# Product-key expert layers: 80 keys weighted in the first stage instead of 64, 48 in the second, and four value tiles loaded early into idle buffers

## The chip, the cores and the metric

The kernel runs on one core of one Trainium2 chip. The metric is the time of one execution on the device in microseconds (us). The core has a matrix engine (TensorE, PE in the rows, with PEld for its weight loads), VectorE (DVE), ScalarE (ACT), GpSimd (POOL) and SyncE (SP), which here issues the loads of weight tiles. The engines run side by side and wait for one another on semaphores.

## The reference, cut to what matters

The kernel computes a network of several layers over 256 tokens of width 1024: a first block, an attention layer, an expert layer, a second attention layer, a second expert layer and a last norm. The change touches only the two expert layers. Each of them computes, for a token `x` (normed):

```python
q = (xc @ w_q).reshape(t, PEER_HEADS, 2, PEER_QDIM // 2)        # 8 heads, 2 halves of 128
sc = jnp.einsum('thpc,hpnc->thpn', q, sub_keys)                  # 128 scores per half
v_half, i_half = lax.top_k(sc, PEER_TOPK_HALF)                   # 16 best of each half
cand = v_half[:, :, 0, :, None] + v_half[:, :, 1, None, :]       # 16 x 16 sums
cand_idx = i_half[:, :, 0, :, None] * PEER_NKEYS + i_half[:, :, 1, None, :]
top_s, pos = lax.top_k(cand, PEER_TOPK)                          # 16 best sums of each head
expert = jnp.take_along_axis(cand_idx, pos, axis=-1)
g = jax.nn.softmax(top_s, axis=-1)
act = jax.nn.gelu(jnp.einsum('thkd,td->thk', u_tab[expert], xc))
return jnp.einsum('thk,thkd->td', g * act, v_tab[expert])
```

There are 128 x 128 experts, so `u_tab` and `v_tab` have 16384 rows each.

## The kernel before, in words

The kernel doesn't gather for most tokens. For 192 of the 256 tokens (`DENSE`) it computes every expert: the first stage multiplies the whole table U, tile by tile, with the tokens and applies Gelu, the hidden values are then multiplied by the weight of each expert (zero for those not picked), and the second stage multiplies them with the whole table V. A tile is 128 x 1024 values, 512 KB, and holds the experts of one first key; each stage has 128 tiles ("keys" below). The other 64 tokens (`GATHERED`) are done by gathering rows: 64 gathers of rows of U (128 x 4 KB each, `row_dot` L2250) and 64 of rows of V (`row_value` L2255). These 128 items lie between the other work of VectorE, in the order that `take(upto)` L2646 and the list `TAKEN` L2297 write out by hand. GpSimd issues gather n when item n - 8 has been taken (eight buffers `gbuf`).

First stage, per key (`experts` L2376): eight matmuls 128 x 192 in fp32 (L2383). SP loads a tile into one of four ring slots as soon as the tile that used the slot is done. ScalarE applies Gelu to each pair of keys (L2494) into `hidden`.

Weights: `one_hots` L2261 builds on VectorE, for a group of 8 tokens, one-hot rows in fp16: `is_first` (L2268), `hot_second` (L2270), and `hot_first` (L2274, twice: `is_first` times the high and the low part of the weight). `weights` L2277 multiplies them on TensorE, 16 matmuls of 128 x 64 per group (L2282), and `weigh` L2287 multiplies the product from PSUM into `hidden` (L2290). Two buffers of each kind alternate. It is done in two halves of the keys: keys 0 to 63 in 24 groups, spread over the last 56 keys of the first stage (`FOUR_AT`, `SIX_AT`), and keys 64 to 127 in 24 groups over the first 53 keys of the second stage. The picks come from `find_picks` L2595 on VectorE. TensorE transposes them (L2392) at key 72, and VectorE turns them to fp16 (L2687 to L2691).

Second stage, per key (`values` L2405): ten matmuls 128 x 512 (fp32r: L2413, L2414, and L344 to L346 in a helper). A V tile is first split by ScalarE into a rounded part (`tile_hi`, L2481 for the first four, L2512 for the others) and by VectorE into the rest (`tile_lo`, L2705), and the hidden values are split alike (L2485, L2486 on ScalarE, L2708 on VectorE); `value_rest` L2702 is L2705 and L2708 together. VectorE stays two keys ahead (`value_rest(a + 2)`). SP loads V tile a into its ring slot: the first four when the U tile in the slot is used, the later ones when VectorE has read the tile (`load_table` L2210).

At the border of the stages ScalarE rounds V tiles 0 and 1 after the last Gelu but one, rounds the hidden values of keys 0 to 3, applies the last Gelu, and rounds V tiles 2 and 3 (L2488 to L2505). VectorE does `value_rest` of keys 0 and 1, the first group of the second half, and then waits for the last Gelu (L2713). In the first expert layer SP clears a list of semaphores between the last load of U and the first of V (L2230 to L2232).

## Time and profile before

| | |
|---|---|
| median of 3 runs | 2077.0 us (2076.82 to 2078.7) |
| profiled execution | 2068.39 us, its span 2066.6 us |
| busy share | TensorE 97%, VectorE 78%, ScalarE 42%, GpSimd 19% |
| first expert layer | first stage from 530.5 us to 880.0 us, second to 1199.6 us |
| second expert layer | first stage from 1392.7 us to 1743.1 us, second to 2056.9 us |

A row of the timeline holds the start, the time that it took, the engine, the line, the operation, and after xN how many of the kind were merged; in brackets stands how long the engine had been idle before it, and what ended the wait. A busy time of TensorE is no measure of how near it is to its peak, since a matmul is counted until its end and the next one begins before that. The distance between starts is. The time around the span is 1.8 us in the profiled execution, and this execution was 8.6 us shorter than the median of the runs.

### The profile page before, as it was taken

The numbers are of one execution on the slowest core, as the hardware profiler recorded it, in microseconds if no ns is written. First come the engines' busy times: TensorE is split into PE (matmuls) and PEld (weight loads), VectorE is DVE, ScalarE is ACT, GpSimd is POOL, SyncE is SP. The second block draws the span as 40 slices with busy tenths as digits, with TensorE's granted clock in tenths as the row PEclk, the third lists the DMA queues.
The fourth block names the chain that finished last, engine by engine and source line by source line (L and its number), as shares of the span: only waits on it lengthen the run. The fifth ranks groups of instructions, "written<-read, shape, count | busy, mean of one in ns | idle before, by whom it ended". The sixth has DMA issues, their size and how long they took to land.

```text
span 2066.6 us, 35237 instructions
## 1 busy us (share of the span) xinstructions
PE 2007.3 (97%) x12408; PEld 1791.5 (87%) x12408; DVE 1622.2 (78%) x3208; ACT 857.9 (42%) x1653; POOL 385.0 (19%) x262
## 2 busy tenths in 40 slices
PE   8999999999999999999999999999999999999998
PEld 6888887779999999977887887899999998778786
DVE  6899886865799276699999967639964756999997
ACT  6557454545101100055565666531101002555665
POOL 0000000000024233303243100000352322232440
PEclk9999999999999999999999999999999999999999
DMA  6554344415389989867799853335998988678995
GB/s 258 198 203 163 114 139 156 138 67 174 133 337 341 368 321 327 300 241 229 262 351 356 294 184 117 113 117 195 391 353 309 346 306 317 224 243 281 371 377 181
DMA packets 132634, 511.17 MB, mean 247 GB/s; under 512 B 15004, under 2 KB 15132, under 8 KB 129856
## 3 DMA queue, kind: packets, MB, share of 16 engines
q1 hardware_dynamic: 95680, 375.81, 51.7%
q0 software_dynamic: 36864, 134.23, 17.6%
q8 instruction: 47, 0.77, 0.1%
q14 instruction: 43, 0.35, 0.1%
HBM read 508.94 MB, written 1.05 MB: 247 GB/s over the span
## 4 chain that ended last, share of the span: by engine, by line
PE 64%; DVE 16%; DMA 5%; issue 2%; ACT 2%; SPq 0%; DVEq 0%; ACTq 0%
PE bank L2383 30%; PE bank L344 8%; PE bank L346 8%; PE bank L345 8%; DVE tile_lo L2705 5%; DMA wbuf<-in_peer_v 3%; PE bank L2413 3%; PE bank L2414 3%; DVE x_tok L2258 2%; DMA wbuf<-in_peer_u 2%; PE bank L2282 1%; DVE w_parts L2708 1%; DVE e_hot_first L2274 1%; DVE e_hidden L2290 1%; DVE tile_lo L274 1%
## 5 line engine op out<-in xcount | busy, mean ns | idle before, releaser
L2383 PE MATMUL bank<-h_dense,wbuf 128*128 128x192 f32 x4096 | 679.7, 327 | 3.7 <-ACT e_stage L2467 2.4
L2383 PEld LDWEIGHTS bank<-h_dense,wbuf 128*128 128x128 f32 x4096 | 664.2, 190 | 6.0 <-issue 4.9
L2512 ACT ACTIVATE tile_hi<-wbuf 128x1024 fp32r<-128x1024 f32 x248 | 263.0, 1060 | 246.1 <-DMA wbuf<-in_peer_v 202.3
L2705 DVE TENSOR_TENSOR tile_lo<-wbuf,tile_hi 128x1024 fp32r<-128x1024 f32 x256 | 311.0, 1215 | 37.7 <-ACT tile_hi L2512 27.4
L2244 POOL DMA_INDIRECT e_gbuf<-in_peer_v,e_row_at x128 | 227.1, 1774 | 484.3 <-DVE x_tok L2258 445.8
L2494 ACT ACTIVATE e_hidden<-bank 128x384 f32<-128x384 f32 x128 | 62.7, 490 | 603.2 <-PE bank L2383 603.2
L2244 POOL DMA_INDIRECT e_gbuf<-in_peer_rows,e_row_at x128 | 155.8, 1218 | 470.1 <-DVE e_dots L2252 239.0
L2413 PE MATMUL bank<-tile_hi,w_parts 128*128 128x512 f32 x512 | 208.5, 407 | 11.1 <-DVE w_parts L2708 10.4
L274 DVE TENSOR_TENSOR tile_lo<-wbuf,tile_hi 128x1024 fp32r<-128x1024 f32 (+2 forms) x117 | 140.3, 1212 | 80.1 <-ACT tile_hi L266 79.2
L2414 PE MATMUL bank<-tile_lo,w_parts 128*128 128x512 f32 x512 | 200.4, 391 | 0.0
L344 PE MATMUL bank<-tile_hi,w_parts 128*128 128x512 f32 x512 | 200.1, 391 | 0.0
L345 PE MATMUL bank<-tile_lo,w_parts 128*128 128x512 f32 x512 | 200.0, 391 | 0.0
L346 PE MATMUL bank<-tile_hi,w_parts 128*128 128x512 f32 x512 | 199.8, 390 | 0.0
L355 PE MATMUL bank<-a_parts,tile_hi 128*128 128x512 f32 x512 | 177.8, 391 | 0.0
L2252 DVE CUSTOM_DVE_ANT_0 e_gbuf<-e_gbuf,x_gathered 128x1024 f32<-128x1024 f32 x128 | 152.2, 1217 | 18.5 <-DMA e_gbuf<-in_peer_rows,e_row_at 18.1
L2258 DVE SCALAR_TENSOR_TENSOR x_tok<-e_gbuf,e_acts,x_tok 128x1024 f32<-128x1024 f32 x128 | 163.4, 1276 | 1.3
L266 ACT ACTIVATE tile_hi<-wbuf 128x1024 fp32r<-128x1024 f32 (+2 forms) x117 | 121.9, 1046 | 66.4 <-PE bank L346 58.9
L354 PE MATMUL bank<-a_parts,tile_hi 128*128 128x256 f32 x512 | 143.8, 281 | 0.6 <-DVE tile_hi L681 0.5
L2413 PEld LDWEIGHTS bank<-tile_hi,w_parts 128*128 128x128 f32 x512 | 96.5, 188 | 42.4 <-DVE w_parts L2708 24.7
L2290 DVE SCALAR_TENSOR_TENSOR e_hidden<-bank,e_hidden 128x512 f32<-128x512 f32 x96 | 65.6, 683 | 80.4 <-PE bank L2282 80.4
L2238 POOL MEMSET x_tok<- 64x1024 f32 x2 | 1.9, 948 | 667.1 <-DVE e_stage L2549 667.1
L561 ACT ACTIVATE tile_hi<-wbuf 128x512 fp32r<-128x512 f32 x144 | 89.9, 630 | 66.6 <-PE bank L355 62.6
(391 smaller groups left out, 3500.3 us busy)
## 6 DMA issues: line engine op xcount, KB each, us to landing
wbuf<-in_peer_u SPq DMA_DIRECT2D x256, 512.0 KB, 5.7
wbuf<-in_peer_v SPq DMA_DIRECT2D x256, 512.0 KB, 5.0
wbuf<-in_w_in SPq DMA_DIRECT2D x16, 2048.0 KB, 7.7
wbuf<-in_peer_q SPq DMA_DIRECT2D x32, 512.0 KB, 3.8
wbuf<-in_hyb_in SPq DMA_DIRECT2D x16, 512.0 KB, 3.7
wbuf<-in_mla_uq SPq DMA_DIRECT2D x9, 512.0 KB, 3.4
wbuf<-in_mla_in SPq DMA_DIRECT2D x8, 528.0 KB, 4.2
wbuf<-in_w_v SPq DMA_DIRECT2D x2, 2048.0 KB, 7.3
```

The costliest lines, as they stand in the source:

```text
L274: nc.vector.tensor_tensor(g["tile_lo"][:, slot, 0:width], g["ring"][:, slot, 0:width], g["tile_hi"][:, slot, 0:width].bitcast(F32), ALU.su ...
L344: nc.tensor.matmul(out, hi[:, cols], other_hi, start=start, stop=False, **kw)
L345: nc.tensor.matmul(out, hi[:, cols], other_lo, start=False, stop=False, **kw)
L346: return nc.tensor.matmul(out, lo[:, cols], other_hi, start=False, stop=stop, **kw)
L355: return nc.tensor.matmul(out, hi[:, cols], parts, start=False, stop=stop, skip_group_check=True)
L2244: nc.gpsimd.indirect_dma_start(out=gbuf[:, b, :], out_offset=None, in_=(U_ROWS if n < SHARED else V_ROWS)[:, :], in_offset=bass.IndirectOf ...
L2258: nc.vector.scalar_tensor_tensor(out=x[:, 1, :], in0=gbuf[:, n % GBUFS, :], scalar=acts[:, n:n + 1], in1=x[:, 1, :], op0=ALU.mult, op1=ALU ...
L2383: last = nc.tensor.matmul(bank[:, j // 2 % 2, j % 2 * S:j % 2 * S + DENSE], ring[:, slot, k * P:(k + 1) * P], h_dense[:, k, :], start=(k = ...
L2413: nc.tensor.matmul(sums(1, c), both, tile_hi[:, slot, cols], start=False, stop=False, skip_group_check=True)
L2414: last = nc.tensor.matmul(sums(1, c), both, tile_lo[:, slot, cols], start=False, stop=False, skip_group_check=True)
L2512: nc.scalar.activation(tile_hi[:, slot, 0:D], ring[:, slot, 0:D], ACT.Copy).then_inc(hi_done, 1)
L2705: nc.vector.tensor_tensor(tile_lo[:, slot, 0:D], ring[:, slot, 0:D], tile_hi[:, slot, 0:D].bitcast(F32), ALU.subtract).then_inc(lo_done, 1)
```

## The change

- Weights: `PARTS` says 80 keys in 32 groups of 6 tokens for the first stage, and 48 keys in 24 groups of 8 tokens for the second. The groups of the first lie in 40 keys from key 80 on (after four of five keys), and 8 keys without a group follow. Those of the second lie in the first 72 keys, one after every third. The transposes of the picks move from key 72 to key 80.
- The two multiplications L2274 become one over an operand of twice the size. High and low part lie interleaved, so that a matmul reads its moving operand with a step of four fp16 values and not of two.
- Items: 86 instead of 78 are taken in the first stage, 6 instead of 10 beside the groups of the second, and the last 36 within 46 keys (72 to 118) instead of 40 within 60 (56 to 116). The Gelu of the gathered dots (L2502) becomes two, after pairs 46 and 51 instead of 54.
- Border: the first four V tiles go to `tile_raw`, which lies where `tile_lo` lies. SP issues these loads directly behind the last of U (in the first expert layer behind the clears), with no wait. The ring loads of V tiles 4 to 7 wait for the last four U tiles. ScalarE rounds V tiles 0 to 3 and the hidden values of keys 0 to 3 ahead of the last Gelu, and only when all four tiles have landed (`v_first`).
- Picks: of the 16 x 16 sums only 17 rows of 8 are kept, and the decoding of places has some more small operations. The zeroing of 64 rows of `x` moves from GpSimd to VectorE, ahead of the first group. The transposes take 128 rows where they took 64.

```diff
+            "tile_raw": nc.alloc_sbuf_tensor_at("tile_raw", [P, SLOTS, TILE], F32, offset=wbuf_at + 2 * BUF),
...
+    PARTS = ((0, 80, 6), (80, 48, 8))
...
-        load_table(sp, V, M_V, used, lo_done)
+        for a in range(SLOTS):
+            sp.dma_start(v_raw[a], V[a:a + 1, :, :].rearrange("a p c -> p (a c)")).then_inc(v_first, DMA)
+        for j in range(SLOTS, STEP):
+            sp.wait_ge(used, M_V + j - STEP + 1)
+            load_slot(sp, V, j, (M_V + j) % SLOTS)
+        load_rest(sp, V, M_V, lo_done)
...
-        for part in range(2):
-            made = nc.vector.tensor_tensor(hot_first[b][:, part, :, :, :], is_first[b][:, :, :, :], pairs(2 + part, HALF), ALU.mult)
-        made.then_inc(hots_done, 1)
+        nc.vector.tensor_tensor(weighted_first, first.unsqueeze(3).to_broadcast([P, pairs, keys, 2, 2]),
+                                pick_parts[:, pairs * n:pairs * n + pairs, :, :].unsqueeze(2).to_broadcast([P, pairs, keys, 2, 2]),
+                                ALU.mult).then_inc(hots_done, 1)
...
-    FOURS, SIXES, WEIGHING = 3, 2, 7
-    FIRST_WEIGHING = ROUNDS - WEIGHING
-    FOUR_AT = {0: 0, 2: 1, 4: 2, 6: 3}
-    SIX_AT = {0: 0, 2: 1, 5: 2, 7: 3, 10: 4, 12: 5}
-    TAKEN, LAST_TAKE = (16, 30, 36, 78, 88), 116
-    EXPS_AT, ACTS_AT = (16, 30), 54
+    FIRST_WEIGHING, FIRST_LOOPS, FIRST_LOOP = FIRST_KEYS // STEP, 2, 20
+    FIRST_AT = {j: n for n, j in enumerate(j for j in range(FIRST_LOOP) if j % 5 < 4)}
+    SECOND_LOOPS, SECOND_LOOP = 3, 24
+    SECOND_AT = {3 * n: n for n in range(8)}
+    WEIGHING = SECOND_LOOPS * SECOND_LOOP // STEP
+    TAKEN, LAST_TAKE = (16, 30, 36, 86, 92), 118
+    EXPS_AT, ACTS_AT, ACTS = (16, 30), (46, 51), (slice(0, 48), slice(48, SHARED))
...
         def rounded_v(a):
-            slot = (M_V + a) % SLOTS
-            act.wait_ge(ring_loaded[slot], DMA * ((M_V + a) // SLOTS + 1))
-            nc.scalar.activation(tile_hi[:, slot, 0:D], ring[:, slot, 0:D], ACT.Copy).then_inc(hi_done, 1)
+            act.wait_ge(v_first, SLOTS * DMA)
+            nc.scalar.activation(tile_hi[:, (M_V + a) % SLOTS, 0:D], v_raw[a], ACT.Copy).then_inc(hi_done, 1)
...
-        for f in range(HALF):
+        for f in range(NKEYS // 2):
+            if f == NKEYS // 2 - 1:
+                act.wait_ge(weighted, 2 + NGROUPS[0])
+                for a in range(SLOTS):
+                    rounded_v(a)
+                    hidden_rounded(a, a)
             act.wait_ge(used, M_U + 2 * f + 2)
-            if f == HALF - 1:
-                act.wait_ge(weighted, 2 + NGROUP)
-                for a in range(SLOTS):
-                    hidden_rounded(a, a)
...
+        nc.vector.memset(x[LOW, 1, :], 0.0).then_inc(picks_kept, 1)
-        dve.wait_ge(bank_free, 2 + HALF // 2)
+        dve.wait_ge(bank_free, 2 + FIRST_KEYS // 2)
```

## Rows read from the trace of the kernel before

**Rows 1.** Timeline of TensorE, end of the first layer's first stage.
```profile
857.32 0.64 PE L2282 MATMUL bank<-e_hot_first,e_hot_second 128*128 128x64 f16 x16
857.81 8.04 PE L2383 MATMUL bank<-h_dense,wbuf 128*128 128x192 f32 x48
...
865.68 0.64 PE L2282 MATMUL bank<-e_hot_first,e_hot_second 128*128 128x64 f16 x16
...
871.45 0.65 PE L2282 MATMUL bank<-e_hot_first,e_hot_second 128*128 128x64 f16 x16
```

**Rows 2.** Timeline of TensorE, second stage: steady keys, last groups, ends.
```profile
1022.76 0.65 PE L2282 MATMUL bank<-e_hot_first,e_hot_second 128*128 128x64 f16 x16
...
1176.93 0.39 PE L2413 MATMUL bank<-tile_hi,w_parts 128*128 128x512 f32 x1
...
1199.37 0.39 PE L346 MATMUL bank<-tile_hi,w_parts 128*128 128x512 f32 x1
...
1884.21 0.65 PE L2282 MATMUL bank<-e_hot_first,e_hot_second 128*128 128x64 f16 x16
...
2056.68 0.39 PE L346 MATMUL bank<-tile_hi,w_parts 128*128 128x512 f32 x1
```

**Rows 3.** Chain in order of time (start, us, what), SP's queue at the border.
```profile
869.19 0.33 SPq L2208
...
875.13 0.34 SPq L2208
```

**Rows 4.** Timeline of ScalarE and TensorE, start of each layer's second stage.
```profile
879.07 1.06 ACT L2481 ACTIVATE tile_hi<-wbuf 128x1024 fp32r<-128x1024 f32 x1 [3.76 <-DMA wbuf<-in_peer_v]
...
884.50 0.80 PE L2413 MATMUL bank<-tile_hi,w_parts 128*128 128x512 f32 x1 [4.52 <-DVE w_parts L2708]
...
1744.52 0.50 PE L2413 MATMUL bank<-tile_hi,w_parts 128*128 128x512 f32 x1 [1.39 <-DVE w_parts L2708]
```

**Rows 5.** Busy time by stretch (PE, PEld, DVE, ACT, POOL, then granted clock, DMA share, GB/s).
```profile
885.00:890.00 5.00, 5.00 (x27) 3.74 (x26) 5.00 (x11) 3.25 (x6) 0.00 (x0) 0.50 0.57 193
...
1050.00:1100.00 50.00, 49.92 (x214) 39.31 (x213) 45.49 (x56) 30.61 (x63) 20.42 (x14) 1.00 0.99 364
1950.00:2000.00 50.00, 49.92 (x218) 40.22 (x217) 48.16 (x59) 31.76 (x66) 26.08 (x15) 1.00 1.00 379
```

**Rows 6.** Timeline of VectorE in the first stage, one group and its items.
```profile
738.39 0.42 DVE L2268 TENSOR_TENSOR e_is_first<-e_wide,e_picks_T 128x512 f16<-128x512 f16 x1
738.73 0.68 DVE L2270 TENSOR_TENSOR e_hot_second<-e_wide,e_picks_T 128x1024 f16<-128x1024 f16 x1
739.34 0.75 DVE L2274 TENSOR_TENSOR e_hot_first<-e_is_first,e_picks_T 128x512 f16<-128x512 f16 x2
741.27 0.69 DVE L2290 SCALAR_TENSOR_TENSOR e_hidden<-bank,e_hidden 128x512 f32<-128x512 f32 x1 [1.18 <-PE bank L2282]
741.87 1.22 DVE L2252 CUSTOM_DVE_ANT_0 e_gbuf<-e_gbuf,x_gathered 128x1024 f32<-128x1024 f32 x1
...
743.01 1.22 DVE L2252 CUSTOM_DVE_ANT_0 e_gbuf<-e_gbuf,x_gathered 128x1024 f32<-128x1024 f32 x1
```

**Rows 7.** Timeline of VectorE in the second stage: a value rest, an item.
```profile
1035.61 1.22 DVE L2705 TENSOR_TENSOR tile_lo<-wbuf,tile_hi 128x1024 fp32r<-128x1024 f32 x1
...
1037.01 1.28 DVE L2258 SCALAR_TENSOR_TENSOR x_tok<-e_gbuf,e_acts,x_tok 128x1024 f32<-128x1024 f32 x1
1038.20 1.22 DVE L2705 TENSOR_TENSOR tile_lo<-wbuf,tile_hi 128x1024 fp32r<-128x1024 f32 x1
```

**Rows 8.** Timeline of VectorE and TensorE where the first group is made.
```profile
720.34 0.36 DVE L2687 TENSOR_SCALAR e_picks_T<-bank 128x192 f16<-128x192 f32 x1 [17.35 <-PE bank L2335]
...
723.28 0.66 PE L2282 MATMUL bank<-e_hot_first,e_hot_second 128*128 128x64 f16 x16 [0.37 <-DVE e_hot_first L2274]
```

**Rows 9.** The page's costliest groups (busy, mean ns), the zeroing on GpSimd.
```profile
L2238 POOL MEMSET x_tok<- 64x1024 f32 x2 | 1.9, 948 | 667.1 <-DVE e_stage L2549 667.1
```

More of the change, by code:

```diff
@@ L2127, in expert_layer @@
     ROUNDS = NKEYS // STEP
-    HALF = NKEYS // 2
-    GROUP = 8
+    PARTS = ((0, 80, 6), (80, 48, 8))
+    FIRST_KEYS = PARTS[0][1]
     WEIGHT_ONE = 4096.0
-    NGROUP = DENSE // GROUP
+    NGROUPS = [DENSE // group for start, keys, group in PARTS]
     TURN_BANKS = (0, 1, 4, 5)
@@ L2277, in weights, with hots @@
-    def weights(pe, half, n, b):
-        pe.wait_ge(hots_done, 2 * (NGROUP * half + n + 1))
-        pe.wait_ge(weighted, NGROUP * half + n + 1)
-        for m in range(GROUP):
+    def hots(half, b):
+        start, keys, group = PARTS[half]
+        first = is_first[b][:, 0:group * keys].rearrange("p (i a m) -> p i a m", a=keys, m=2)
+        weighted_first = hot_first[b][:, 0:2 * group * keys].rearrange("p (i a w m) -> p i a w m", a=keys, w=2, m=2)
+        second = hot_second[b][:, 0:group * NKEYS].rearrange("p (i a m) -> p i a m", a=NKEYS, m=2)
+        return first, weighted_first, second
@@ new lines, in one_hots, with by_pairs @@
+    def one_hots(dve, half, n):
+        start, keys, group = PARTS[half]
+        pairs = group // 2
+        first, weighted_first, second = hots(half, n % 2)
+        tokens = slice(group * n, group * n + group)
+        def by_pairs(rows, keys):
+            return picks_T[:, rows, tokens].rearrange("p (i m) -> p i m", m=2).unsqueeze(2).to_broadcast([P, pairs, keys, 2])
+        nc.vector.tensor_tensor(first, wide[:, start:start + keys, :].unsqueeze(1).to_broadcast([P, pairs, keys, 2]),
+                                by_pairs(0, keys), ALU.is_equal).then_inc(first_done, 1)
+        nc.vector.tensor_tensor(second, wide[:, :, :].unsqueeze(1).to_broadcast([P, pairs, NKEYS, 2]),
+                                by_pairs(1, NKEYS), ALU.is_equal).then_inc(hots_done, 1)
+        dve.wait_ge(first_done, NGROUPS[0] * half + n + 1)
+        nc.vector.tensor_tensor(weighted_first, first.unsqueeze(3).to_broadcast([P, pairs, keys, 2, 2]),
+                                pick_parts[:, pairs * n:pairs * n + pairs, :, :].unsqueeze(2).to_broadcast([P, pairs, keys, 2, 2]),
+                                ALU.mult).then_inc(hots_done, 1)
@@ L2281, in weights @@
+    def weights(pe, half, n, b):
+        start, keys, group = PARTS[half]
+        first, weighted_first, second = hots(half, b)
+        pe.wait_ge(hots_done, 2 * (NGROUPS[0] * half + n + 1))
+        pe.wait_ge(weighted, NGROUPS[0] * half + n + 1)
+        for m in range(group):
             for part in range(2):
-                last = nc.tensor.matmul(bank[:, 2 + b, m * HALF:(m + 1) * HALF], hot_second[b][:, m // 2, :, m % 2],
-                                        hot_first[b][:, part, m // 2, :, m % 2],
+                last = nc.tensor.matmul(bank[:, 2 + b, m * keys:(m + 1) * keys], second[:, m // 2, :, m % 2],
+                                        weighted_first[:, m // 2, :, part, m % 2],
@@ L2499, in scalar @@
                 exps(1, 0)
-            if f == ACTS_AT:
-                act.wait_ge(gather_used, GATHER_0 + SHARED)
-                nc.scalar.activation(acts[:, :], dots[:, :], ACT.Gelu).then_inc(exps_done, 1)
-            if f >= HALF - 2:
-                for a in range(2):
-                    rounded_v(2 * (f - HALF + 2) + a)
+            if f in ACTS_AT:
+                part = ACTS[ACTS_AT.index(f)]
+                act.wait_ge(gather_used, GATHER_0 + part.stop)
+                nc.scalar.activation(acts[:, part], dots[:, part], ACT.Gelu).then_inc(exps_done, 1)
         def value_tile(r, j):
@@ L2716, in vector @@
             value_rest(a + 2)
[L2717 to L2719 removed]
+            if a < WEIGHING * STEP and a % SECOND_LOOP in SECOND_AT:
+                if done < NGROUPS[1] - 1:
                     one_hots(dve, 1, done + 1)
```

144 lines of the change are left out of this document (71 added, 73 removed).

## The prediction, made before the changed kernel was run

> **What bounds the kernel now.** I read the page first: TensorE is busy 97% of the span, so only what TensorE does, or what makes it wait, can move the end. As busy time hides gaps, I then read distances between starts on TensorE's timeline. In the first stage three keys and one group of weight matmuls take 865.68 - 857.32 = 8.36 us, two keys and a group 871.45 - 865.68 = 5.77 us [rows 1]. So a key costs 2.6 us and a group 0.56 us, of which 0.49 us lies between its start and that of the next key's matmuls, 30 ns for each of 16. In the second stage ten steady keys last from 1176.93 to 1199.37 plus one matmul, 22.65 us [rows 2], so 2.265 us a key. With these two prices I measured what the second stages lose. From the first value matmul to the 24th group lie 53 keys and 23 groups, by the prices 120.0 + 11.3 = 131.3 us. They took 1022.76 - 884.50 = 138.3 us in the first expert layer and 1884.21 - 1744.52 = 139.7 us in the second: 7.0 and 8.4 us lost [rows 2, 4]. From there to the end one group and 75 keys should take 170.4 us and took 176.8 and 172.7 us: 6.4 and 2.3 us lost [rows 2]. Between the stages TensorE idles 4.52 and 1.39 us [rows 4]. That is all there is to win: 4.5 + 7.0 + 6.4 and 1.4 + 8.4 + 2.3, 30 us in both layers. The first stages run nearly without gaps.
>
> Three causes stand behind the loss. VectorE: per group of the second stage it does two value rests (1.40 us each, from 1035.61 to 1037.01 [rows 7]), one-hots of 0.34 + 0.61 + 0.67 us and a weighing of 0.60 us [rows 6], together 5.0 us, plus an item of 1.19 us [rows 7] at every sixth key. TensorE needs 2 x 2.265 + 0.49 = 5.02 us. So VectorE binds there. The clock: after the idle 4.5 us of the first layer the granted clock is 0.50, which is 1.2 GHz, from 885 to 890 us [rows 5], and the first key takes twice its time (2.6 us more, part of the 7.0). Late in the stage: transfers. With two items in three keys the queues must bring 1.667 tiles of 0.524 MB in 2.265 us, 386 GB/s, and the rows show 364 and 379 GB/s at a share of 0.99 and 1.00 [rows 5].
>
> **The change, part by part, for each layer.**
>
> *Weight matmuls.* 24 groups of 16 with 64 columns become 32 of 12 with 80, and 24 of 16 with 64 become 24 of 16 with 48. If columns set the 30 ns, 16 more cost 6.7 ns at 2.4 GHz: a group of the first stage costs 12 x 37 ns + 0.07 = 0.51 us, so 32 x 0.51 - 24 x 0.56 = +2.9 us, and the second stage saves 24 x 16 x 6.7 ns = 2.6 us. If loading the stationary operand sets it, 32 x (0.36 + 0.07) - 13.4 = +0.4 us, and nothing is saved. Both give +0.4, which I take. The ends are -2.2 (load price in the first, column price in the second) and +2.9 (the reverse). The Trainium skill (TensorE: Matmul & The Clock Gate, "Wait — 56ns, not 53.3ns?") gives N / 2.4 GHz + 2.5 ns with a floor of 25 ns. By that the estimate would be +2.5 and -1.6, net +0.9 us a layer. At 64 columns it says 29 ns and the trace 30 ns.
>
> *First stage, VectorE.* Where the row shows 0.34 us for 512 elements and 0.61 for 1024, the price is 0.07 us + elements / 1920 per us [rows 6]. A new group: 480 (0.32) + 768 (0.47) + 960 (0.57) + weighing of 480 at one element a cycle (0.57) = 1.93 us. Items: 28 dots at 1.14 (741.87 to 743.01 [rows 6]) and 22 values at 1.19 [rows 7], 58.1 us over 32 groups, 1.82 a group. Sum 3.75 us. TensorE: 1.25 keys and a group, 3.25 + 0.51 = 3.76 us. Equal, so VectorE has no reserve left, where it had 1.18 us of idle time in a group before [rows 6]. The start costs more: from the first conversion to the first group lie 2.94 us, 0.37 of them waited for by TensorE [rows 8]. Zeroing on VectorE is added; GpSimd needs 0.95 us [rows 9], I take 1.1, and the first one-hots are 0.25 us shorter: 0.85 more. I add 0.25 us for uneven gaps between groups. So +1.1 us, between +0.3 and +4.
>
> *What has no price at the end.* The shorter search for picks ends in the 17.35 us that VectorE waits for the transposes [rows 8]. Without that cover its few us would count. Wider transposes are 11 times some 0.06 us, and the split Gelu removes a wait on VectorE that TensorE didn't feel. Earlier gathers only fill buffers earlier.
>
> *Border.* SP has queued: last load of U, in the first layer the clears, then four loads of V. The clears stay: 869.19 to 875.13, 5.9 us [rows 3]. The last U load is issued 10.3 us before the stage's end T (four keys remain). First layer: V is issued from T - 4.4. One tile took 3.9 us (875.13 to 879.07 [rows 3, 4]), three more follow at 0.524 MB / 370 GB/s = 1.4 us, so all have landed at T + 3.3. ScalarE waits for all four; behind its wait stand only the last Gelu and all rounding. Rounding 1.06, VectorE's 1.14 + 0.36 and some handover give 2.6 us: TensorE starts at T + 5.9, against 4.5 now. The clock falls as before: 2.6, and 0.3 for small waits. Sum 8.8, before 4.5 + 7.0 = 11.5: -2.7 us. Second layer: V is issued at T - 9.9, behind the last U tile, landed at about T - 1.2, TensorE starts at T + 1.4, as now. Then VectorE is late three times: the first group's one-hots (0.5), rests of key 2 (0.15) and of key 3 (0.9), as it waits for the last Gelu behind 6.2 us of rounding on ScalarE. Sum 3.0, before 1.4 + 8.4 = 9.8: -6.8 us. In both I take nothing for the rest of the 72 keys: VectorE needs 3 x 1.40 + (0.27 + 0.60 + 0.47 + 0.47) + 0.3 = 6.3 us, and TensorE 3 x 2.265 + 0.4 = 7.2 us. Ends: 2 us either way in each layer, by the landing time.
>
> *Late items.* From key 72 there are 36 items in 46 keys, and the first 28 of them each call a gather: 0.783 a key. VectorE needs 1.40 + 0.783 x 1.19 = 2.33 us against 2.265, at most 3 us in all, most of it covered by its lead of two keys: loss 1 us, the lower end. Transfers: 36 + 28 tiles in 36 keys, 33.6 MB in 81.5 us = 412 GB/s. At 364 GB/s that lasts 92.2 us, at 379 88.5 us: losses 10.7 and 7.0, the upper ends. Full slots and eight full buffers at the start absorb some. I take 8.0 and 5.5, near the transfer bound, since the stretch already loses at 386 GB/s: +1.6 and +3.2 us.
>
> *Sum.* First layer 0.4 + 1.1 - 2.7 + 1.6 = +0.4; second 0.4 + 1.1 - 6.8 + 3.2 = -2.1. Together -1.7 us. The profiled execution would go from 2068.4 to 2066.7 us; it was 8.6 us below the median, so I apply the same difference to the median: 2077.0 - 1.7 = 2075.3 us.
>
> **The rivals.**
>
> *The late stretch loses no more than VectorE's 1 us.* Then 7.0 and 4.5 us more are won: -13.2, 2064 us; half of it gives 2069. For it: the second layer lost only 2.3 us at a demand of 386. Against it: the share of 0.99 to 1.00.
>
> *Transfers at their full price, and matmuls at +2.9.* 0.4 + 2.5 + 2.7 = +5.6 and -2.1 + 2.5 + 1.5 = +1.9: +7.5, 2084.5 us.
>
> *Slower by one mechanism: the joined multiplication runs at one element a cycle.* It is the only operation of a new shape, with four dimensions and two of them repeated. It would take 0.07 + 1.00 instead of 0.57 us. From 3.76 us a group VectorE sets the pace of the weighing part of the first stage; 4.25 us is above it by 0.49, 32 times in two layers: +31, 2107 us. Against it: both old inputs also step by pairs of adjacent values, and the rows show two elements a cycle.
>
> *The wider step of the moving operand costs TensorE.* At half the column rate: 32 x 12 x 37 ns + 24 x 16 x 23 ns = 23 us a layer, 2121 us. Against it: at the present step of 4 bytes the 30 ns leave 3 ns above the columns. No row shows 8 bytes. The Trainium skill (SBUF — State Buffer, on cachelines of 16 bytes) holds two accesses to a line to be enough for full rate, and a step of 8 bytes makes just two; one more would cost.
>
> **How the numbers follow.** Forecast 0.42 (own range 2071 to 2080), late stretch free 0.36, full transfer and matmul price 0.12, slow multiplication 0.06, slow step 0.04. The likeliest gives 2075.3. For 8 in 10 I reach into the two neighbours: 2063 to 2085, which leaves out 0.10 above by the last two and as much again in the tails. About 0.2%, 4.2 us, can be told from no change. Faster: 0.36 + 0.06 = 0.42. Slower: 0.10 + 0.10 + 0.01 = 0.21. Within: 0.37.
>
> **What would show it.** Right: weight groups of 0.51 us in the first stage and about 0.4 in the second, three keys and a group 7.2 us apart from key 4 to 72, no idle VectorE between groups of the first stage, 5 to 6 us idle with a clock of 0.50 after it in the first layer and under 2 us in the second, and key distances of 2.4 to 2.5 us from key 72 to 108 with ScalarE waiting for V tiles. Wrong: groups of the first stage 4.2 us apart, an early start of the second stage in the first layer, or late keys at 2.27 us.

## The result, and the profile after

The changed kernel takes 2120.7 us (median, 2117.1 to 2122.5) where the kernel before takes 2077.9 us beside it. The ratio is 1.0194 with an interval of 1.0163 to 1.0226, so it is slower by 43 us. Its profiled execution took 2121.6 us, with a span of 2119.8 us, against 2068.4 and 2066.6 before. The profile before is 9.5 us shorter than the median beside which the changed kernel was timed, so a difference of these two profiles overstates the change. A second comparison of the same kernel (experiment 5 below) gave 1.0176 [1.0144, 1.0208] and a profiled span of 2104.7 us. The forecast was 2075.3 us, the range ended at 2085, and the mechanism that decided, at 2121 us, had been given a chance of 0.04.

The weight matmuls of the first stage answer [rows 1]. Timeline of TensorE, changed kernel:

```profile
755.27 1.05 PE L2301 MATMUL bank<-e_hot_first,e_hot_second 128*128 128x80 f16 x12 [1.12 <-DVE e_hot_first L2290]
756.14 2.82 PE L2406 MATMUL bank<-h_dense,wbuf 128*128 128x192 f32 x16
758.79 1.05 PE L2301 MATMUL bank<-e_hot_first,e_hot_second 128*128 128x80 f16 x12
```

Twelve matmuls of 80 columns take 756.14 - 755.27 = 0.87 us up to the next key's first, 72.5 ns each. Before, sixteen of 64 took 0.49 us, 30 ns each. In the second stage the same view answers [rows 2, 4]:

```profile
913.31 0.80 PE L2435 MATMUL bank<-tile_hi,w_parts 128*128 128x512 f32 x1 [5.54 <-DVE w_parts L2739]
...
917.75 0.94 PE L2301 MATMUL bank<-e_hot_first,e_hot_second 128*128 128x48 f16 x16
918.51 0.62 PE L2435 MATMUL bank<-tile_hi,w_parts 128*128 128x512 f32 x1
...
1796.07 0.80 PE L2435 MATMUL bank<-tile_hi,w_parts 128*128 128x512 f32 x1 [2.47 <-DVE w_parts L2739]
```

Sixteen matmuls of only 48 columns take 0.76 us here and 0.72 us in the steady part: 45 ns each, where fewer columns than before should have taken less than 30. VectorE is not the one behind it. Its timeline answers [rows 6]:

```profile
758.20 0.40 DVE L2285 TENSOR_TENSOR e_is_first<-e_wide,e_picks_T 128x480 f16<-128x480 f16 x1
758.52 0.55 DVE L2287 TENSOR_TENSOR e_hot_second<-e_wide,e_picks_T 128x768 f16<-128x768 f16 x1
758.99 0.64 DVE L2290 TENSOR_TENSOR e_hot_first<-e_is_first,e_picks_T 128x960 f16<-128x960 f16 x1
759.88 0.66 DVE L2310 SCALAR_TENSOR_TENSOR e_hidden<-bank,e_hidden 128x480 f32<-128x480 f32 x1 [0.25 <-PE bank L2301]
```

The joined multiplication of 960 elements is busy for 0.64 us, as the 1024 elements of the second one-hot were before (0.68), and 0.57 us pass to the next operation where one follows at once, as forecast: it kept the fast rate. And VectorE now waits for TensorE again (0.25 us).

All stages, from distances between starts on TensorE's timeline (us; first and second expert layer). "Group" is from a group's first matmul to the next key's. "Idle" is counted from the last matmul of the first stage, taken as long as the distance between its like, so it is 0.1 to 0.2 us more than in the brackets of the rows:

| kernel | first stage | idle at border | second stage | group, first / second stage | both layers |
|---|---|---|---|---|---|
| before | 349.4, 350.3 | 4.6, 1.5 | 315.1, 312.4 | 0.49 / 0.49 | 1333.3 |
| changed, first profile | 375.7, 371.0 | 5.7, 2.6 | 316.4, 314.1 | 0.87 / 0.72 | 1385.5 |
| changed, second profile | 364.9, 366.1 | 6.1, 2.7 | 314.8, 314.4 | 0.87 / 0.72 | 1368.9 |
| changed, step of 4 bytes | 354.8, 353.6 | 6.6, 3.4 | 307.2, 304.8 | 0.44 / 0.42 | 1330.3 |
| best (experiment 5) | 353.5, 353.0 | 0, 0 | 302.9, 302.9 | 0.45 / 0.42 | 1312.3 |

The first profile of the changed kernel holds 16.6 us in these layers that the second does not. They are the subject of experiment 5.

### The profile page after: what moved, and what is told of

The parts are those of the page before. It is cut to its first block, busy times and chain, and to the rows that moved or that the text cites. A ratio compares the mean times of both kernels' runs of the same rounds, so it can differ in the third digit from the quotient of the medians.

```text
span 2119.8 us, 35225 instructions
## 1 busy us (share of the span) xinstructions
PE 2051.8 (97%) x12408; PEld 1838.7 (87%) x12408; DVE 1604.7 (76%) x3192; ACT 860.7 (41%) x1655; POOL 364.1 (17%) x260
## 4 chain that ended last, share of the span: by engine, by line
PE 75%; DVE 6%; DMA 4%; issue 2%; ACT 2%; another core or an unknown queue 1%; SPq 0%; DVEq 0%; ACTq 0%
PE bank L2406 28%; PE bank L345 10%; PE bank L347 10%; PE bank L346 10%; PE bank L2435 5%; PE bank L2436 5%; PE bank L2301 4%; DMA wbuf<-in_peer_u 2%; DMA wbuf<-in_peer_v 1%; DVE tile_lo L275 1%; DVE x_tok L2264 1%; DMA tile_raw<-in_peer_v 1%; PE bank L2391 1%; DVE tile_lo L2736 1%
## 5 line engine op out<-in xcount | busy, mean ns | idle before, releaser
L2406 PE MATMUL bank<-h_dense,wbuf 128*128 128x192 f32 x4096 | 686.8, 328 | 13.7 <-DMA wbuf<-in_peer_u 9.0
L2736 DVE TENSOR_TENSOR tile_lo<-wbuf,tile_hi 128x1024 fp32r<-128x1024 f32 x248 | 302.4, 1219 | 12.1 <-ACT tile_hi L2527 9.9
L2250 POOL DMA_INDIRECT e_gbuf<-in_peer_v,e_row_at x128 | 211.5, 1653 | 536.7 <-DVE x_tok L2264 510.1
L267 ACT ACTIVATE tile_hi<-wbuf 128x1024 fp32r<-128x1024 f32 (+2 forms) x117 | 121.9, 1046 | 64.2 <-PE bank L347 59.6
L2310 DVE SCALAR_TENSOR_TENSOR e_hidden<-bank,e_hidden 128x480 f32<-128x480 f32 (+1 forms) x112 | 68.6, 612 | 73.9 <-PE bank L2301 68.9
L682 DVE TENSOR_TENSOR tile_hi<-wbuf,tile_hi 128x512 fp32r<-128x512 f32 x144 | 98.4, 688 | 24.5 <-ACT tile_hi L562 23.6
```

What stands on the lines that cost most here:

```text
L2250: nc.gpsimd.indirect_dma_start(out=gbuf[:, b, :], out_offset=None, in_=(U_ROWS if n < SHARED else V_ROWS)[:, :], in_offset=bass.IndirectOf ...
L2406: last = nc.tensor.matmul(bank[:, j // 2 % 2, j % 2 * S:j % 2 * S + DENSE], ring[:, slot, k * P:(k + 1) * P], h_dense[:, k, :], start=(k = ...
L2736: nc.vector.tensor_tensor(tile_lo[:, slot, 0:D], raw, tile_hi[:, slot, 0:D].bitcast(F32), ALU.subtract).then_inc(lo_done, 1)
```

## The experiments

**1. The step of the moving operand, undone and done alone.** The theory after the result: TensorE reads the interleaved operand with a step of four fp16 values (8 bytes), and that halves its column rate. The rival: the new split of keys, the border or the transfers cost the 43 us. The first kernel is the changed one with high and low part apart again, so that the step is 4 bytes:

```diff
-        weighted_first = hot_first[b][:, 0:2 * group * keys].rearrange("p (i a w m) -> p i a w m", a=keys, w=2, m=2)
+        weighted_first = hot_first[b][:, 0:2 * group * keys].rearrange("p (w i a m) -> p w i a m", w=2, a=keys, m=2)
...
-                                        weighted_first[:, m // 2, :, part, m % 2],
+                                        weighted_first[:, part, m // 2, :, m % 2],
```

> The changed kernel with one thing put back: high and low part of the weight lie apart again and are made by two multiplications, so a weight matmul reads its moving operand with a step of 2 fp16 values (4 bytes) and not of 4 (8 bytes). Groups, keys, items and border stay as changed. Theory 1 (the step halves the column rate): a group of 12 x 80 falls from 0.87 us to about 0.45 us and one of 16 x 48 from 0.72 to about 0.40 us, 32 x 0.42 + 24 x 0.32 = 21 us a layer, 42 us in all, so about 2078 us. Theory 2 (80 columns in 32 groups are dear in themselves, whatever the step): groups stay at 0.87 us and 0.72 us, within 5 us of 2121. Theory 3 (VectorE sets the pace): its work grows by 0.07 us a group, so a little slower than 2121.

Measured: 2068.7 us, ratio 0.9998 [0.9971, 1.0025]. Timeline of TensorE in this kernel:

```profile
752.81 0.60 PE L2300 MATMUL bank<-e_hot_first,e_hot_second 128*128 128x80 f16 x12
753.26 2.84 PE L2405 MATMUL bank<-h_dense,wbuf 128*128 128x192 f32 x16
755.93 0.61 PE L2300 MATMUL bank<-e_hot_first,e_hot_second 128*128 128x80 f16 x12
...
904.98 0.58 PE L2300 MATMUL bank<-e_hot_first,e_hot_second 128*128 128x48 f16 x16
905.39 0.48 PE L2434 MATMUL bank<-tile_hi,w_parts 128*128 128x512 f32 x1
```

The groups are down to 0.45 us (37 ns a matmul) and 0.41 us (26 ns). A key and a group of the first stage take 3.12 us instead of 3.53. With nothing changed but the layout and one multiplication made two, the whole slowdown is gone. (The two kernels were timed in different comparisons, each beside the kernel before, so their ratios are set side by side and not their times.)

The second kernel is the one before with only the interleaved layout and the joined multiplication:

```diff
-        for part in range(2):
-            made = nc.vector.tensor_tensor(hot_first[b][:, part, :, :, :], is_first[b][:, :, :, :], pairs(2 + part, HALF), ALU.mult)
+        nc.vector.tensor_tensor(hot_first[b][:, :, :, :, :], is_first[b][:, :, :, :].unsqueeze(3).to_broadcast([P, PAIRS, HALF, 2, 2]),
+                                pick_parts[:, PAIRS * n:PAIRS * n + PAIRS, :, :].unsqueeze(2).to_broadcast([P, PAIRS, HALF, 2, 2]),
...
-                                        hot_first[b][:, part, m // 2, :, m % 2],
+                                        hot_first[b][:, m // 2, :, part, m % 2],
```

> The kernel before with one thing of the change: the two multiplications joined, high and low part interleaved, so the step of the moving operand is 8 bytes; 64 columns, 16 matmuls a group, 24 groups in each half as before. Theory 1: a matmul of 64 columns goes from 30 ns to about 58 ns, a group from 0.49 to 0.93 us, 48 x 0.44 = 21 us a layer, about 2119 us. Theory 2 (column count and grouping): no change, 2077 us. Theory 3 (VectorE): VectorE saves 0.07 us a group, no change.

Measured: 2101.8 us, ratio 1.0143 [1.0108, 1.0178]. Timeline of TensorE, first stage:

```profile
762.12 1.14 PE L2283 MATMUL bank<-e_hot_first,e_hot_second 128*128 128x64 f16 x16
763.08 5.11 PE L2384 MATMUL bank<-h_dense,wbuf 128*128 128x192 f32 x30
```

A group takes 0.96 us, twice the 0.49 of [rows 1]. The first stages grow by 11.1 and 10.4 us, which is the full price of 24 x 0.47 = 11.3. The second stages grow by 1.6 and 8.0 only. Their first 72 keys grow by 7.4 and 6.4 us of 11.3: there VectorE was the slower one, and part of the slower matmuls lies beside its work. The rest is no saving of that kind. In the first layer the idle at the border is 1.8 us and not 4.6, and keys 72 to 118 take 104.7 us where the profile before has 110.5, with the same items in the same order. One profile of each kernel doesn't tell why. So the layers lose 28 us where 42 were expected from the two stages (45 by the measured group). Both directions agree: the step is the cause.

**2. The step by itself.** A kernel of its own with 48 matmuls in a row for each setting, between single matmuls of 512 columns (line 50) as marks.

> Only matmuls, nothing of the reference: for each of 48, 64, 80 and 128 columns of fp16, 48 matmuls in a row with a moving step of 1, 2, 3, 4, 6 and 8 values, then a step of 4 at three other offsets, two steps of the stationary operand, and fp32 with steps of 1, 2 and 4. Theory 1 says that the time from start to start jumps between a step of 2 and of 4 values, from columns / 2.4 GHz to twice that (64 columns: 30 to about 57 ns; 80 columns: 37 to 72 ns). If it is a question of 16-byte lines touched in a row, a step of 3 should lie between and 8 should be twice 4 again; if it is a simple rate of half for any step over 4 bytes, 3, 4, 6 and 8 are alike. Theory 2 says all steps are alike at a given column count.

Timeline of TensorE. A setting lasts from its first start to that of the mark behind it:

```profile
22.30 1.36 PE L45 MATMUL bank<-mh,wh 128*128 128x48 f16 x48
23.50 0.38 PE L50 MATMUL bank<-mh,wh 128*128 128x512 f16 x1
...
27.06 2.33 PE L45 MATMUL bank<-mh,wh 128*128 128x48 f16 x48
29.21 0.40 PE L50 MATMUL bank<-mh,wh 128*128 128x512 f16 x1
...
62.48 2.00 PE L45 MATMUL bank<-mh,wh 128*128 128x80 f16 x48
64.31 0.38 PE L50 MATMUL bank<-mh,wh 128*128 128x512 f16 x1
...
67.46 3.68 PE L45 MATMUL bank<-mh,wh 128*128 128x80 f16 x48
70.96 0.40 PE L50 MATMUL bank<-mh,wh 128*128 128x512 f16 x1
...
121.28 3.06 PE L45 MATMUL bank<-mh,wh 128*128 128x64 f16 x48
124.16 0.40 PE L50 MATMUL bank<-mh,wh 128*128 128x512 f16 x1
```

48 columns take (23.50 - 22.30) / 48 = 25.0 ns at a step of 2 bytes and 44.8 at 8 bytes; 80 columns take 38.1 ns at 4 bytes and 72.9 at 8. In ns from start to start, with the granted clock of the stretch in brackets where it was below 0.99 (the 38.1 ns hold a first moment at the low clock; over the whole 1.83 us it was 0.96):

| step | 48 columns | 64 | 80 | 128 |
|---|---|---|---|---|
| 2 bytes | 25.0 | 53.5 (0.50) | 66.7 (0.50) | 80.0 (0.69) |
| 4 bytes | 25.0 | 45.8 (0.60); 30.2 | 38.1 | 57.9 |
| 6 bytes | 35.4 | 45.8 | 56.5 | 88.3 |
| 8 bytes | 44.8 | 59.6; 60.0 (0.51) | 72.9 | 115.6 |
| 12 bytes | 66.3 | 86.5 | 108.3 | 171.2 (0.84) |
| 16 bytes | 86.3 (0.79) | 116.0 (0.50) | 143.5 (0.50) | 226.7 (0.50) |

From 80 to 128 columns one more column costs (57.9 - 38.1) / 48 = 0.41 ns at 4 bytes, which is one cycle of 2.4 GHz, then 0.66 at 6 bytes, 0.89 at 8, 1.31 at 12 and 1.73 at 16. Up to 4 bytes the cycle sets the price. Beyond, the price is in proportion to the step, some 0.22 ns for every two bytes of it: 3 x 0.22 at 6 bytes, 4 x 0.22 at 8, 8 x 0.22 at 16. The 72.9 and 44.8 ns are those of the groups in the changed kernel (72.5 and 45). The entry of 60.0 ns is the setting from 121.28 on, with the operand one value further, and it is as long at 0.51 of the clock as its like at 1.00 (59.6). Busy time by stretch (PE, PEld, DVE, POOL, then granted clock, DMA share, GB/s):

```profile
121.40:124.13 2.73, 2.73 (x49) 2.73 (x48) 0.00 (x0) 0.00 (x0) 0.51 0.00 0
124.50:127.21 2.71, 2.71 (x49) 2.71 (x47) 0.00 (x0) 0.00 (x0) 1.00 0.00 0
```

So a wide step is limited by something that does not follow the engine's clock. Where it sits between memory and engine these runs don't tell. A very wide step also goes with a lower clock. TensorE was busy throughout, yet the granted clock fell to 0.50 four times, each time in a setting of 12 or 16 bytes, and came back to 1.00 in a setting of 2 to 8 bytes. In the same columns, 80 columns at 16 bytes and 128 at 4 bytes:

```profile
76.90:83.64 6.74, 6.74 (x49) 5.94 (x48) 0.00 (x0) 0.00 (x0) 0.50 0.00 0
...
88.20:90.83 2.63, 2.63 (x48) 2.63 (x47) 0.00 (x0) 0.00 (x0) 1.00 0.00 0
```

In the changed kernel, where groups at 8 bytes lie between other matmuls, the clock stayed at 1.00 (750 to 900 us of its second profile). (The 30.2 ns of the table are those of a setting whose stationary operand has a step of 4 bytes too.)

**3. The search for picks.** The changed kernel at a step of 4 bytes, with the old search over 16 x 16 sums:

```diff
+            work = half_scores[:, t, :, :].rearrange("p j n -> p (j n)").rearrange("p (h a b) -> p h a b", h=PH, a=PK)
...
-            after(nc.vector.tensor_tensor(sums_of[:, :, 0:PK], by_half[:, :, 0, 0:1].to_broadcast([P, PH, PK]), by_half[:, :, 1, :], ALU.add))
```

> As after_step4b, and the old search over 16 x 16 sums and the old decoding are back, so that the gathers of the first expert layer start some 4 us later again. In the changed kernel TensorE idled 3.8 us at 595 us for a U tile that SP issued 5 us late at the turn of its loop, while the gathers' first burst ran, and the clock fell behind it; that was not so before. If the earlier gathers are the cause, this kernel is 5 to 8 us faster than after_step4b. If the late issue is chance, the two are within 2 us of each other.

Measured: 2065.3 us, ratio 0.9985 [0.9962, 1.0008], against 0.9998 with the new search on the same chip. The intervals overlap, so no gain of the shorter search is seen, as forecast. In neither profile does TensorE wait 3.8 us for a U tile as it did in the changed kernel, so this pair can't tell what brought that wait (experiment 5 takes it up).

**4. The border and the late items.** Four kernels in a comparison of their own, beside a kernel before of 2080.5 us, so their ratios are compared with one another only. (All four take 217 to 222 us to their first group, where two kernels of experiments 1 and 3 take 213 to 215 with the same work, so first stages are not compared across the two. Experiment 5 comes back to this.) All have the step of 4 bytes. The first has the old border: V tiles through the ring, rounding around the last Gelu.

```diff
-        for a in range(SLOTS):
-            sp.dma_start(v_raw[a], V[a:a + 1, :, :].rearrange("a p c -> p (a c)")).then_inc(v_first, DMA)
-        for j in range(SLOTS, STEP):
-            sp.wait_ge(used, M_V + j - STEP + 1)
+        for j in range(STEP):
+            sp.wait_ge(used if j < SLOTS else lo_done, M_V + j - SLOTS + 1)
```

> after_step4b with the border of the kernel before: V tiles 0 to 3 go to the ring when their U tile is used, ScalarE rounds two of them after the last Gelu but one and two after the last. In after_step4b TensorE idles 6.6 us between the stages of the first expert layer and 3.4 us in the second (4.6 and 1.5 before), the first four keys take 11.9 and 10.9 us (13.0 and 12.0 before) and the second stages 307.2 and 304.8 us (315.1 and 312.4 before). Theory 1: the early loads gave next to nothing, since all four must land before the first is rounded; the second stage is shorter because its groups ask less of VectorE and TensorE. Then the gaps go back to 4.6 and 1.5 us, the first four keys to about 13 and 12, the rest stays, and the time is within 3 us of after_step4b. Theory 2: the early loads carry the gain of the second stage. Then the second stages go back to 312 to 315 us and the time rises by 10 us or more.

Measured: 2071.6 us, ratio 0.9953 [0.9936, 0.9969]. TensorE idles 1.5 and 1.2 us here at the borders, against 6.6 and 3.4 us with the early loads and the joint wait in experiment 1: those made the border worse. Timelines of ScalarE and TensorE, old border:

```profile
891.13 1.06 ACT L2493 ACTIVATE tile_hi<-wbuf 128x1024 fp32r<-128x1024 f32 x1 [4.14 <-DMA wbuf<-in_peer_v]
...
894.27 0.50 PE L2430 MATMUL bank<-tile_hi,w_parts 128*128 128x512 f32 x1 [1.41 <-DVE w_parts L2736]
```

The run missed what was expected of it: an idle of 4.6 us was to come back in the first layer, and it is 1.5, with the old border. In the profile of the kernel before, the second V tile was ready for ScalarE 3.5 us after the first (882.60 and 879.07 us), here 1.2 us after it (892.37 and 891.13). The second kernel of experiment 1, which has the old border and the old order of the items, shows 1.3 us (898.59 and 897.29) and an idle of 1.8 us. So a late second tile made the 4.6 us of the profile before, and neither the border nor the order of the items makes it come every time. Why it came late there is open. The forecast took these 4.5 us for a lasting loss.

In the changed kernel ScalarE waits for four tiles instead of one. Its timeline, and of the chain in order of time the three pieces ahead of it:

```profile
910.67 1.06 ACT L2497 ACTIVATE tile_hi<-tile_raw 128x1024 fp32r<-128x1024 f32 x1 [7.57 <-DMA tile_raw<-in_peer_v]
```

```profile
903.01 0.34 SPq L2238
...
903.87 0.43 SPq L2238
...
904.34 6.24 DMA tile_raw<-in_peer_v
```

The loads are issued behind the clears, from 903.01 to 904.3, and the last lands 6.24 us later. The next kernel gives each tile a semaphore of its own:

```diff
-            sp.dma_start(v_raw[a], V[a:a + 1, :, :].rearrange("a p c -> p (a c)")).then_inc(v_first, DMA)
+            sp.dma_start(v_raw[a], V[a:a + 1, :, :].rearrange("a p c -> p (a c)")).then_inc(v_each[a][0], DMA)
...
-            act.wait_ge(v_first, SLOTS * DMA)
+            act.wait_ge(v_each[a][0], DMA * v_each[a][1])
```

> after_step4b, and ScalarE waits for each of the four early V tiles by itself, not for all four. The tiles land some 1.3 us apart. Theory 1 (the joint wait makes the gap): the first rounding starts 3 to 4 us earlier in both layers, the gaps fall from 6.6 to about 3 us and from 3.4 to under 1 us, the clock doesn't fall at the second layer's border, 5 to 8 us in all. Rival: the gap is set by the issue of the loads, the first tile lands hardly before the fourth as they share the queues, and less than 2 us is won.

Measured: 2068.2 us, ratio 0.9940 [0.9917, 0.9963]. The idle of the second layer is gone, that of the first is 2.1 us, more than with the old border:

```profile
891.31 1.06 ACT L2497 ACTIVATE tile_hi<-tile_raw 128x1024 fp32r<-128x1024 f32 x1 [3.97 <-DMA tile_raw<-in_peer_v]
...
893.95 0.50 PE L2435 MATMUL bank<-tile_hi,w_parts 128*128 128x512 f32 x1 [1.94 <-DVE w_parts L2738]
```

The third kernel issues the four loads ahead of the clears as well (the same two lines moved up in SP's program).

> each_tile, and in the first expert layer SP issues the four early V tiles before it clears its list of semaphores, which takes 5.9 us, and not after. Theory 1: the gap of the first layer falls to under 1 us and no clock falls behind it, 4 to 6 us faster than each_tile, with the second layer as it was. Rival: the clears now delay the ring loads of V tiles 4 to 7 and the loss only moves there, so that keys 4 to 8 stall, no gain.

Measured: 2065.4 us, ratio 0.9929 [0.9905, 0.9952], and no idle at either border. ScalarE's timeline has the rounding begun at 886.40 and the last Gelu at 891.81, so its wait of 1.53 us is over before TensorE needs anything:

```profile
886.40 1.06 ACT L2497 ACTIVATE tile_hi<-tile_raw 128x1024 fp32r<-128x1024 f32 x1 [1.53 <-DMA tile_raw<-in_peer_v]
...
891.81 0.47 ACT L2511 ACTIVATE e_hidden<-bank 128x384 f32<-128x384 f32 x1
```

The three intervals overlap, so the traces have to tell. Idle time and first 72 keys, both layers together: 364.3 us with the joint wait (experiment 1), 355.3 with the old border, 356.1 with a wait for each tile, 352.4 with the clears moved too. So the joint wait lost 9 us, a wait for each tile alone got back to the old border and no further, and only with the clears behind the loads are 2.9 us won. Keys 72 to 118 took 2.6 us more in that last kernel than with the old border (107.3 and 107.4 against 105.8 and 106.3), which hides the gain in the total. The fourth kernel spreads the later items again:

```diff
-    TAKEN, LAST_TAKE = (16, 30, 36, 86, 92), 118
+    TAKEN, LAST_TAKE = (16, 30, 36, 84, 104), 118
```

> each_tile_clears with the items spread anew: 84 in the first stage, 20 beside the groups of the second (72 keys), and 24 instead of 36 in keys 72 to 118. Keys 72 to 118 took 106.4 and 104.9 us in after_step4b, 104.2 by their price. Theory 1 (transfers bind late): the late stretch falls to 104.3 in both layers, the 72 keys before it stay as they were since VectorE needs 7.1 us for three keys and TensorE 7.3: 2 to 3 us faster. Rival: VectorE binds in the 72 keys, which grow by more than 3 us.

Measured: 2057.1 us, ratio 0.9884 [0.9860, 0.9908]. Keys 72 to 118 take 104.3 us in both layers where they took 107.3 and 107.4 in the kernel before it; 46 keys at 2.265 us are 104.2. Its interval touches that of the kernel before it (0.9905 to 0.9908), but its five times (2055.0 to 2061.5) all lie below that kernel's six (2062.6 to 2070.3).

**5. The changed kernel and the best one, side by side.** Two things were open. In the first profile of the changed kernel SP's queue had stood still for 11.3 us in all, the longest time for 5.0 us while the first gathers ran, and TensorE idled behind it. Waits of SP's queue, changed kernel, first profile (us in total, times, longest):

```profile
SPq L2211 <- remote: 11.3, 3, 5.0
```

And the best kernel and the changed one had not been timed beside each other. Both kernels are unaltered.

> The changed kernel once more, unaltered. Open from its first profile: the queue of SyncE stood 5.0 us at a turn of its loop while the first gathers ran (from 586.5 us), TensorE idled 0.7 and 3.8 us behind it, and 223.3 us passed from the start of the first stage of the first expert layer to its first weight group, where the same kernel with a step of 4 bytes took 214.5. If the slow step is the only lasting cost, this run shows no such stop, at most 216 us to the first group, weight groups at 0.87 and 0.72 us from their start to the next matmul as before, and a ratio of 1.015 to 1.020. If the stop belongs to the order of the work in this kernel (another cause beside the step), it comes again at the same loop turn, with 220 us or more to the first group.

> Step of 4 bytes, a wait for each V tile, the clears behind the early loads, and the later items spread as before: the best kernel so far, now beside the changed kernel on one chip. By the causes named so far it is 42 us (step) plus 2 x 3 (gap at the border) plus 2 x 1.5 to 3 (late stretch) below the changed kernel, some 52 us, and its ratio to the kernel before is near 0.990. A ratio above 0.997 would mean that its gain in the first comparison came from the chip and not from the edits.

Measured: the changed kernel 2105.3 us, ratio 1.0176 [1.0144, 1.0208]; the best one 2048.6 us, ratio 0.9909 [0.9880, 0.9937]. In the second profile of the changed kernel SP has no wait of that kind, and the first groups begin 212.9 and 213.7 us after the start of the stage, where it had been 223.3 and 218.3. Of the 16.6 us between the two profiles of the changed kernel, 10.4 + 4.6 = 15.0 lie ahead of the first groups. So the stop is no lasting part of this kernel. But it was no accident of one execution either: the same wait stands in all four profiles of experiment 4, first at 581 to 585 us, where it was 586.5 in the changed kernel. The one with the old border:

```profile
SPq L2210 <- remote: 22.8, 7, 4.4
```

None of the five profiles of experiments 1, 3 and 5 that hold the whole kernel has it, nor has the profile of the kernel before. It goes with the comparison and not with the kernel. In the two comparisons where it is seen, the kernel before takes 2077.9 and 2080.5 us, in the other two 2067.8 and 2068.4; and all four times of the changed kernel are 2117.1 to 2122.5 beside the first of these and 2101.5 to 2108.4 beside the last. The ratio hardly moves, 1.0194 and 1.0176. The one profile of the kernel before has no such wait, but that execution was 8.6 us shorter than the median of its runs; whether the others held the wait is not shown. What held SP is open. The two kernels here are 56.8 us apart, with 52 expected.

Timelines of TensorE and ScalarE in the best kernel at the first border, which answer [rows 4]:

```profile
882.84 3.41 PE L2406 MATMUL bank<-h_dense,wbuf 128*128 128x192 f32 x20
885.95 0.53 PE L2435 MATMUL bank<-tile_hi,w_parts 128*128 128x512 f32 x1
```

```profile
881.71 1.06 ACT L2497 ACTIVATE tile_hi<-tile_raw 128x1024 fp32r<-128x1024 f32 x1
```

The first value matmul follows the last hidden one with no idle time, because ScalarE had begun on the first tile 4.2 us earlier. In the second stage this kernel loses nothing: 128 x 2.265 + 24 x 0.53 = 302.6 us, and it takes 302.9.

## Why the prediction was wrong, point by point

**The step that failed** is the price of the weight matmuls, "30 ns for each of 16" carried over by columns or by loads. Neither of its two prices held for the new access. The mechanism was named as a rival and held at 0.04 on two grounds: that a step of 4 bytes costs nothing, which says nothing about 8, and the rule in the Trainium skill (SBUF — State Buffer) that two accesses to a line of 16 bytes are enough for the full rate. The runs contradict that rule for a moving operand: at 6 bytes the rate is already down to 0.41 / 0.66 of the full one, at 8 bytes, two accesses to a line, to half. The rival's size was near. It gave 23 us a layer. Against the kernel with 4 bytes, both layers together, the second profile shows 1368.9 - 1330.3 = 38.6 us, 19 a layer: 10.1 and 12.5 in the first stages (32 groups, a period of 3.53 against 3.12 us, make 13.1) and 7.6 and 9.6 in the second, less 0.5 and 0.7 at the borders. That its 2121 us meet the measured 2120.7 is in part luck: 46 us for the step were too much against 38.6. "No row shows 8 bytes" was a reason to keep the chance well above 0.04. A change that alters the access of 1536 matmuls on the bounding engine has its price in doubt first of all.

**The rest of the sum came out, in part by luck.** Without the step the changed kernel is at 0.9998; the forecast of -1.7 us meant 0.9992. But its terms missed and cancelled, both layers together: the border, forecast at -9.5 us, gave -3.7, and the late items, forecast at +4.8, gave -5.8. The terms, from the row "step of 4 bytes" against "before":

- *Weight matmuls.* The two prices were columns (+2.9 in the first stage, -2.6 in the second) or loads (+0.4 and nothing). Columns set it: 37 ns at 80, 26 ns at 48. With what a group does to the key behind it, a group costs 3.117 - 2.600 = 0.517 us (0.51 forecast) where it cost 0.563, so 32 x 0.517 - 24 x 0.563 = +3.0. In the second stage it costs 0.53 us where it cost 0.60 before (5.14 us for two keys and a group where nothing waits), so -1.7. Net +1.3, taken as +0.4. The Trainium skill (TensorE: Matmul & The Clock Gate, "Wait — 56ns, not 53.3ns?"), N / 2.4 GHz + 2.5 ns and no less than 25, agrees with these runs at steps up to 4 bytes within 2.3 ns (25.0 at 48 columns, 38.1 at 80, 57.9 at 128), and its estimate of +0.9 was nearer than mine; it does not speak of the step.
- *VectorE in the first stage*, +1.1. The first stages grew by 5.4 and 3.3 us, 4.4 on average, where 2.9 + 1.1 = 4.0 was forecast at the price by columns. Right. The new operations cost what was worked out: 0.32, 0.47 and 0.57 us.
- *Joined multiplication at one element a cycle*: fell, as the rows above show.
- *Border, first layer.* Forecast 5.9 us of idle time, measured 5.7 to 6.6. Right, for the reason given: the clears, then four tiles. In the second layer 1.4 was forecast and 2.6 to 3.4 measured: tiles behind the last of U landed later than I took, inside the end of 2 us. Idle time and loss in the first 72 keys together are 8.4 and 4.3 us, where 8.8 and 3.0 were forecast. The term still missed, since the loss before, from which it was counted, held some 2.5 us a layer that were the groups' own price (below), and an idle time of 4.5 us that the same border does not show each time (experiment 4). What I did not see is that the idle time of the second layer can bring the clock down there too. Busy time by stretch in the changed kernel (PE, PEld, DVE, ACT, POOL, then granted clock, DMA share, GB/s), to set beside [rows 5], and ahead of them that of the kernel before at its second border, where the clock stayed up:

```profile
1744.50:1749.50 5.00, 4.52 (x33) 3.52 (x34) 3.58 (x7) 2.70 (x7) 0.00 (x0) 1.00 1.01 403
```

```profile
915.00:920.00 5.00, 5.00 (x29) 3.79 (x29) 4.43 (x9) 2.99 (x7) 0.00 (x0) 0.62 0.00 1
...
1797.00:1802.00 5.00, 5.00 (x30) 3.90 (x29) 4.43 (x10) 3.75 (x10) 0.00 (x0) 0.75 0.09 34
```

How long the engine idled does not decide this alone. With the step of 4 bytes the second layer's idle time was 3.24 us by the profile, and the clock stayed up. With the old search for picks it was 3.23 us, and the clock fell. With a wait for each tile it fell after 1.94 us, in the first layer. These three in this order:

```profile
1748.80:1753.80 5.00, 4.73 (x34) 3.67 (x35) 4.49 (x10) 4.60 (x12) 0.00 (x0) 1.00 0.13 48
```

```profile
1747.40:1752.40 5.00, 5.00 (x29) 3.78 (x30) 4.49 (x10) 4.14 (x10) 0.00 (x0) 0.66 0.15 59
```

```profile
893.95:898.95 5.00, 5.00 (x29) 3.82 (x30) 4.49 (x10) 4.67 (x12) 0.00 (x0) 0.66 1.03 419
```

- *Loss to VectorE in the second stage.* The gain came: the second stages at 4 bytes are 7.9 and 7.6 us shorter. It comes from one group in three keys, not from the early loads, since the old border has it too (305.3 and 305.7 us). Of the 7.0 and 8.4 us that I called lost, about 2.5 were the price of the groups themselves, which I had put at 0.49 us where they cost 0.60 with the slower start of the next key.
- *Late items.* Over-estimated. Forecast losses were 8.0 and 5.5 us, measured are 106.4 and 104.9 us for keys 72 to 118 against 104.2, so 2.2 and 0.7, and in the changed kernel's second profile 1.7 and 1.8. The wrong step was to take 364 and 379 GB/s as what the queues can give, and the 6.4 us lost in the first layer as the cost of such a demand. The kernel before with only the step widened (experiment 1) has the same items in these keys and loses 0.5 us there (and 3.7 in the second layer). The changed kernel moves more in the first layer's late keys (second profile):

```profile
1095.00:1125.00 30.00, 30.00 (x134) 24.87 (x133) 29.76 (x36) 18.00 (x39) 15.60 (x11) 1.00 1.00 379
1125.00:1155.00 30.00, 30.00 (x134) 24.83 (x133) 29.54 (x37) 17.61 (x37) 14.73 (x10) 1.00 1.01 393
1155.00:1185.00 30.00, 29.92 (x130) 23.65 (x129) 29.98 (x36) 18.73 (x39) 14.58 (x9) 1.00 1.01 394
```

With the DMA engines' share at 1.00 the rate still rose to 394 GB/s (and to 419 for 5 us at the border, in the last row of the point on the border), and TensorE waited next to nothing. VectorE is busy for 89.3 of 90 us there, so it is as near to being the bound as the transfers, as the forecast's lower end had it. No run separates the two: moving items away eases both. The best kernel asks for less in the same keys:

```profile
1070.00:1100.00 30.00, 30.00 (x134) 24.84 (x133) 26.83 (x34) 19.20 (x41) 11.76 (x7) 1.00 0.94 348
1100.00:1130.00 30.00, 30.00 (x134) 24.87 (x133) 25.52 (x33) 17.52 (x37) 11.81 (x7) 1.00 0.95 351
```

So the "late stretch free" rival (0.36) described this part better than the forecast did.

## What to carry to other kernels

When an edit changes how the bounding engine reads an operand, measure that access by itself before pricing the rest: one multiplication saved on VectorE cost 1536 slower matmuls on the engine that sets the time. Keep the moving operand of TensorE at 4 bytes from value to value or less, and interleave along another axis. Where several tiles are awaited at a border, give each its own wait and issue the loads ahead of anything slow in the same queue. Here early loads with one joint wait lost 9 us against loads at the old time, and with both remedies they won 2.9. And before a profile is compared with another one, look whether both hold the same disturbances: 15 us lay ahead of the first groups in one profile of the changed kernel and not in the other, more than any term of this forecast.
